# Weight slots of even attention and retention as 512-column pairs, a two-part gate product, and moved waits

## The reference, cut to what matters

```python
def even_layer(x, g_norm, w_in, b_f, w_out):
    z = rms_norm(x, g_norm) @ w_in
    ...
    log_f = jax.nn.log_sigmoid(fa.astype(f32) + b_f.astype(f32))
    ya = forgetting_attention(hA(qa), hA(ka), hA(va), log_f).reshape(Bsz, S, WIDTH_FOX)
    yb = dilated_attention(hB(qb), hB(kb), hB(vb)).reshape(Bsz, S, WIDTH_DIL)
    y = jnp.concatenate([ya * jax.nn.silu(ga), yb * jax.nn.silu(gb)], axis=-1)
    return x + y @ w_out

def odd_layer(x, g_norm, w_in, w_out):
    z = rms_norm(x, g_norm) @ w_in
    q, k, v, g = jnp.split(z, [qk_w, 2 * qk_w, 2 * qk_w + v_w], axis=-1)
    ...
    y = retention(q, k, v.reshape(Bsz, S, N_HEADS_RET, RET_V_DIM))
    y = head_group_norm(y).reshape(Bsz, S, v_w).astype(x.dtype)
    return x + (y * jax.nn.silu(g)) @ w_out
```

## Time and profile before

| | |
|---|---|
| runs, us | 1420.81, 1422.55, 1423.06 (median 1422.55) |
| the profiled execution's own time, us | 1422.35 |
| its span, first to last instruction, us | 1420.5 |
| mean granted TensorE clock | 0.994 |
| TensorE busy | 1374.0 us, 97% |
| VectorE, ScalarE, GpSimd busy | 976.5, 764.2, 96.6 us |
| weights loaded | 279 slots of 1 MB, median 4.9 us from issue to landing |

### The profile page before, as it was taken

The page is one execution under the profiler, slowest core; times in us unless marked ns, Lnnn a source line. Parts: engine busy times, 40 slices in busy tenths (PEclk is TensorE's granted clock), DMA queues, the critical chain, the costliest instruction groups (busy, mean ns, idle before and its releaser), DMA issues.

```text
span 1420.5 us, 22649 instructions
## 1 busy us (share of the span) xinstructions
PE 1374.0 (97%) x9089; PEld 1217.5 (86%) x9089; DVE 976.5 (69%) x1369; ACT 764.2 (54%) x927; POOL 96.6 (7%) x114
## 2 busy tenths in 40 slices
PE   7999999999999999999999999999999999999996
PEld 7998998789988889878999889887787888888884
DVE  6546566465766477866544475868887898898887
ACT  5545488334323317734433336743676677677673
POOL 0000032100001110001222010001000000000000
PEclk9999999999999999999999999999999999999998
DMA  7544333446543535534555535541898989889996
GB/s 272 216 161 144 123 145 137 161 149 216 199 149 119 212 136 181 178 120 173 193 190 185 181 147 215 180 159 54 334 347 303 347 327 345 334 327 351 335 335 248
DMA packets 44106, 306.36 MB, mean 216 GB/s; under 512 B 4912, under 2 KB 5168, under 8 KB 8176
## 3 DMA queue, kind: packets, MB, share of 16 engines
q1 hardware_dynamic: 41760, 296.22, 56.7%
q0 software_dynamic: 2256, 8.88, 1.8%
HBM read 304.03 MB, written 1.05 MB: 215 GB/s over the span
## 4 chain that ended last, share of the span: by engine, by line
PE 78%; DVE 10%; ACT 4%; DMA 4%; issue 3%; POOL 1%; DVEq 0%; SPq 0%; ACTq 0%
PE g_ps L585 18%; PE g_ps L587 18%; PE g_ps L586 18%; PE a_ps L585 5%; PE a_ps L587 5%; PE a_ps L586 5%; PE a_ps L590 4%; DMA raw<-w_dram 4%; DVE w_lo L1611 3%; ACT w_hi L1264 2%; PE a_ps L594 2%; PE o_ps L590 2%; DVE x L1742 1%; DVE tiny L1658 1%; POOL tiny L493 1%
## 5 line engine op out<-in xcount | busy, mean ns | idle before, releaser
L1611 DVE TENSOR_TENSOR w_lo<-raw,w_hi 128x2048 fp32r<-128x2048 f32 x239 | 546.3, 2289 | 226.1 <-ACT w_hi L1264 224.8
L1264 ACT ACTIVATE w_hi<-raw 128x2048 fp32r<-128x2048 f32 x239 | 457.3, 1914 | 259.7 <-DMA raw<-w_dram 101.8
L585 PE MATMUL g_ps<-x_hi,w_hi 128*128 128x256 f32 x880 | 252.2, 287 | 0.0
L586 PE MATMUL g_ps<-x_lo,w_hi 128*128 128x256 f32 x880 | 249.6, 284 | 0.0
L587 PE MATMUL g_ps<-x_hi,w_lo 128*128 128x256 f32 x880 | 249.5, 283 | 0.0
L585 PE MATMUL g_ps<-w_hi,x_hi 128*128 128x256 f32 (+1 forms) x672 | 230.5, 343 | 7.8 <-DVE w_lo L1611 3.9
L587 PE MATMUL g_ps<-w_hi,x_lo 128*128 128x256 f32 (+1 forms) x672 | 225.2, 335 | 0.0
L586 PE MATMUL g_ps<-w_lo,x_hi 128*128 128x256 f32 (+1 forms) x672 | 224.9, 335 | 0.0
L585 PEld LDWEIGHTS g_ps<-x_hi,w_hi 128*128 128x128 f32 x880 | 169.4, 193 | 4.0 <-issue 3.5
L586 PEld LDWEIGHTS g_ps<-x_lo,w_hi 128*128 128x128 f32 x880 | 169.5, 193 | 0.0
L587 PEld LDWEIGHTS g_ps<-x_hi,w_lo 128*128 128x128 f32 x880 | 169.4, 192 | 0.0
(11 more groups left out here) (326 smaller groups left out, 2043.4 us busy)
## 6 DMA issues: line engine op xcount, KB each, us to landing
raw<-w_dram SPq DMA_DIRECT2D x279, 1024.0 KB, 4.9
arena<-rows_dram POOLq DMA_DIRECT2D x3, 1024.0 KB, 5.1
arena<-xT_dram SPq DMA_DIRECT2D x2, 512.0 KB, 4.7
x<-x_dram SPq DMA_DIRECT2D x2, 512.0 KB, 10.4
extra<-extra_dram POOLq DMA_DIRECT2D x1, 1024.0 KB, 6.5
extra<-rows_dram POOLq DMA_DIRECT2D x2, 512.0 KB, 4.1
y_spare<-rows_dram POOLq DMA_DIRECT2D x4, 256.0 KB, 4.7
out_dram<-x SPq DMA_DIRECT2D x4, 256.0 KB, 2.1
```

The lines of the kernel that those rows point to most:

```text
L585: pe.matmul(ps, lh, rh, start=start, stop=False, skip_group_check=True)
L586: pe.matmul(ps, lh, rl, start=False, stop=False, skip_group_check=True)
L1264: act.activation(w_hi[w_place(s)][:, :], raw[PLACE[s]][:, :], ACT.Copy).then_inc(hi_done, 1)
L1611: dve.tensor_tensor(w_lo[w_place(s)][:, :], raw[PLACE[s]][:, :], w_hi[w_place(s)][:, :].bitcast(F32), ALU.subtract).then_inc(lo_done, 1)
```

## The change

It does these things:

- **Pairs.** Slots 20 to 23, 40 to 47 and 56 to 63 are laid out in DRAM as 4 x 128 rows by 512 columns (`wide_slots`), two slots a pair. `wide_slot(s, half)` uses one of them: for each of the two token tiles 4 x 3 matmuls of 512 columns, each tile into a bank of its own; a slot has 24 matmuls in place of 48. Both banks of a pair are copied after its second slot. For slots 40 and 41 both copies stand ahead of ScalarE's two splits; for later pairs the even slot's split stands ahead of the copies.
- **Retention.** VectorE takes a head's moments as soon as its output is there, then the next head's `decayed`, the norm, and only then the weight split and the gates; gates go in pairs, and each covers one token tile by 512 columns. `turn_outputs` waits for both gates of its pair.
- **Waits of attention.** The three waits ahead of each of the four attentions go; each pair of heads waits for the copy of its own K (and V) slot.
- **Narrow product.** It becomes `small_rows(0, 0)`: 32 matmuls of 128 columns with 48 or 24 weight columns, a copy of 48 rows by ScalarE (after `even_slot(3)`, ahead of `even_slot(4)`), and `fold_rows(0)` on TensorE between slots 4 and 5. VectorE splits slot 8 ahead of the log gates.
- **Start.** ScalarE runs a one-column copy before its first wait on a load.
- **Last mixer norm.** VectorE takes `low_part(5, 0)` after `finish(5, 1)`; TensorE has 8 filling matmuls and the transposes of tile 1 ahead of the first router part, where it had the part and 4 filling matmuls.
- **Loop counts.** `round_counts` moves from behind the split of slot 145 to right behind the first `select`; its one wide step stays behind.

```diff
+                         first=True, last=True, k_ready=copied(at_k + p // 2),
+                         v_ready=copied(at_v + p // 4 * 2 + 1 if b else p // 2)) for p in range(HF // 2)]
...
+            def wide_mm(s, half, t, ks):
+                w = weights(s + half, (4, 512))
+                for k in ks:
+                    mm = parts_mm(g_ps[bank_of(s + t)][:, :], pick(from_x, lambda u: u[:, k, t * P:(t + 1) * P]),
+                                  pick(w, lambda u: u[:, k - 4 * half, :]), k == 0, k == KD - 1)
+                return mm
+            def wide_free(s, t):
+                if g_nth[s + t] > 0:
+                    pe.wait_ge(g_free[bank_of(s + t)], g_nth[s + t])
+            def wide_slot(s, half):
+                pe.wait_ge(lo_done, s + half + 1)
+                for t in range(NT):
+                    if half == 0:
+                        wide_free(s, t)
+                    mm = wide_mm(s, half, t, range(4 * half, 4 * half + 4))
+                mm.then_inc(used, 1)
...
 begin(i, first), no second:
-                    first(0, every)
-                    keep_busy(4, 2, G_ALL)
+                    keep_busy(8, 2, G_ALL)
                     for b in range(2):
                         turn_rows_of(i, 1, b)
+                    first(0, every)
                 first(1, every)
...
-            narrow_product(0, HF)
-            for s in range(4, 8):
+            for t in range(NT):
+                small_rows(0, 0)(t, range(KD))
+            even_slot(4)
+            fold_rows(0)
+            for s in range(5, 8):
                 even_slot(s)
...
-            for s in range(9, 12):
-                pe.wait_ge(g_free[bank_of(s)], g_nth[s] + 1)
...
-                pe.wait_ge(r_y, b + 1)
+                pe.wait_ge(r_y, b - b % 2 + 2)
...
 ScalarE
+            act.wait_ge(pool_own, 3)
+            act.activation(tiny[:, 246:247], zero_col[:, :], ACT.Copy)
             act.wait_ge(ident_in, 16)
...
             for s in range(1, 4):
                 even_slot(s)
+            act.wait_ge(narrow_full, 1)
+            act.activation(rows24, a_ps[0][0:48, 0:S], ACT.Copy).then_inc(rows_copied, 1)
+            even_slot(4)
             act.wait_ge(f_in, 1)
...
             for m in range(8):
-                copy_slot(OD_V + m, rv[:, :, m * S:(m + 1) * S])
+                if m % 2:
+                    act.wait_ge(used, OD_V + m + 1)
+                    for t in range(NT):
+                        j = bank_of(OD_V + m - 1 + t)
+                        act.activation(rv[:, t, (m - 1) * S:(m + 1) * S], g_ps[j][:, :], ACT.Copy).then_inc(g_free[j], 1)
+                    for n in ((m - 1, m) if m == 1 else (m,)):
+                        ahead(OD_V + n)
+                elif m:
+                    ahead(OD_V + m)
...
 VectorE, rest_of_norm
-                low_part(i, 0)
+                if i < 5:
+                    low_part(i, 0)
                 centre(i, 1)
                 finish(i, 1)
+                if i == 5:
+                    low_part(i, 0)
...
 VectorE, retention
             for h in range(RH):
-                for u in G_AFTER[h]:
-                    ahead(OD_G + u)
-                    while gated <= u and gated < 2 * h:
-                        gate_slot(gated)
-                        gated += 1
+                dve.wait_ge(r_out, h + 1)
+                stats_of(lambda t: [a_ps[1 + t][:, :]], EPS)
                 if h < RH - 1:
                     decayed(h + 1)
-                dve.wait_ge(r_out, h + 1)
-                moments(lambda t: [a_ps[1 + t][:, :]], EPS)
                 y = inverse_root()
...
                 ins.then_inc(r_norm, 1)
+                for u in G_AFTER[h]:
+                    ahead(OD_G + u)
+                    while (gated | 1) <= u and gated < 2 * h + 2:
+                        gate_slot(gated)
+                        gated += 1
...
 VectorE, experts
                 select(slice(0, 2), 0)
+                round_counts()
                 ahead(L_WO[1] + 2)
```

More of the change, by code:

```diff
@@ L625, in rows_slot @@
                 mm.then_inc(used, 1)
[L627 to L641, removed]
             def out_mm(s, order, n, t, rows_ready=None):
@@ L686, in parts_come, with wide_part, part_of @@
                     pe.wait_ge(n_lo, 4 * i + 2 * t + k // 4 + 1)
+            def wide_mm(s, half, t, ks):
[14 more added lines that the diff above has]
+                mm.then_inc(used, 1)
+            def wide_part(i, s, half):
+                def part_of(t, ks):
+                    if t == 0 and ks[0] == 0:
+                        pe.wait_ge(lo_done, s + half + 1)
+                    if half == 0 and ks[0] == 0:
+                        wide_free(s, t)
+                    if ks[0] == 0:
+                        pe.wait_ge(n_lo, 4 * i + 2 * t + half + 1)
+                    mm = wide_mm(s, half, t, [4 * half + k // 2 for k in ks if k % 2 == 0])
+                    if t == 1:
+                        mm.then_inc(used, 1)
+                return part_of
             def token_part(i, s):
@@ L851, in even_slot @@
             def even_slot(s):
-                (token_slot if s in range(EV_V[0], EV_V[0] + 4) or s in range(EV_V[1], EV_V[1] + 4) else rows_slot)(s)
+                if s in range(EV_V[1], EV_V[1] + 4):
+                    wide_slot(s - s % 2, s % 2)
+                else:
+                    rows_slot(s)
             def plain_slot(s):
@@ L1331, in even_slot @@
                     ins = act.activation(gate_even(s - EV_G[0]), g_ps[bank_of(s)][:, :], ACT.Silu)
+                elif b and m >= 8:
+                    if s % 2:
+                        for t in range(NT):
+                            r = s - 1 + t
+                            ins = act.activation(qkv[1][2][t][:, (m - 8) // 2 * 512:(m - 8) // 2 * 512 + 512],
+                                                 g_ps[bank_of(r)][:, :], ACT.Copy)
+                            ins.then_inc(g_free[bank_of(r)], 1)
+                    ahead(s)
+                    return
                 elif s - EV_V[b] in range(4):
@@ L1395, in gate_slot @@
             def gate_slot(u):
-                s = OD_G + u
-                act.wait_ge(used, s + 1)
-                if u >= 3:
-                    act.wait_ge(r_y, u - 2)
-                act.activation(gate_view(s), g_ps[bank_of(s)][:, :], ACT.Silu).then_inc(g_free[bank_of(s)], 1)
-                ahead(s)
+                act.wait_ge(used, OD_G + u + 1)
+                for e in ((u - 1, u) if u % 2 else ()):
+                    s = OD_G + e
+                    if e >= 3:
+                        act.wait_ge(r_y, e - 2)
+                    act.activation(gate_view(s), g_ps[bank_of(s)][:, :], ACT.Silu).then_inc(g_free[bank_of(s)], 1)
+                ahead(OD_G + u)
             gate_slot(0)
```

81 lines of the change are left out of this document (35 added, 46 removed).

## The result

| | before | changed |
|---|---|---|
| runs, us | 1420.81 to 1424.99, median 1422.8 (4) | 1407.16 to 1410.64, median 1408.26 (4) |
| ratio | | 0.990, 95% interval 0.9884 to 0.9917 |
| the profiled execution's own time, us | 1422.35 | 1410.64 |

What follows compares the result with a forecast made beforehand. TensorE, with 78% of the chain, was taken to bound the kernel. Pairs 6.0 + retention 2.6 + attention waits 3.2 - start 1.9 + norm and experts 5.1 = 15.0 us faster: median 1407.4, own range 1404 to 1411.

Steps and rivals of the forecast that it cites:

- Pairs: Twenty slots as 512-column matmuls: 0.30 us saved a slot, 6.0 us in all, between 5.0 and 7.0.
- Rival 3: Pairs: width saves nothing, a matmul costs only its columns; 1.2 of 6.0 us remains, 1412 us; chance 0.05.
- No wait of TensorE at a pair's second tile: Sign for the pairs: TensorE never waits for the second tile's bank, since 12 matmuls (2.7 us) cover its copy.
- rival 4: Pairs: the bank of a pair's second tile is freed late, making the kernel slower, 1427 us at 2.0 a pair; chance 0.03.
- Retention, order: Retention stage: with moments ahead of VectorE's split, the waits before the second to fourth output products go, 1.7 us.
- Retention, odd output: End of retention: TensorE's 1.02 us wait for GpSimd's part of two outputs shrinks, 0.9 us gained.
- Waits of attention: Ahead of the four attentions: waits of 3.5 us go, a few tenths stay; 3.2 us gained, between 2.0 and 3.5.
- Start: Start up to slot 8: 1.9 us slower, with a 4.8 us wait before the fold and a clock fall costing 1.5.
- Rival 1: Start: ScalarE makes the 48-row copy in time, no new wait or clock fall; start gains 4.4, 1401 us; chance 0.08.
- The fall at 41.92: Start, kernel before: half clock for 3.41 us after 16-column matmuls, 1.7 us lost; should go with the narrow product.
- Norm, counts and experts: Last norm to slot 147: 0.4 us from the norm, 3.4 from an earlier load, 1.7 from the clock; 5.1 quoted.
- rival 2: Experts: loads at 0.95 share set the pace, about 1 of 5.1 us is kept, 1411.5 us; chance 0.14.

Runs made afterwards that it cites:

- c_after: The changed kernel itself, unaltered, measured once more in a second series against the kernel before: median 1408.28 us, ratio 0.989.
- after: The changed kernel as first measured against the kernel before: median 1408.26 us, ratio 0.990; its profiled execution took 1410.64 us.
- e6_narrow_v: Changed kernel with the retention's eight V slots (40 to 47) again as 48 matmuls of 256 columns, copied slot by slot: 1409.99 us, ratio 0.9903.
- e5_copies_first: Changed kernel with ScalarE's two copies of every retention V pair ahead of both the pair's splits: 1408.82 us, ratio 0.9883 to the kernel before.
- e4_old_order: Changed kernel with VectorE's old retention order, weight split and gates ahead of the decay and moments: 1412.78 us, ratio 0.9914 to the kernel before.
- e8_x_first: Changed kernel with ScalarE's 48-row copy ahead of `even_slot(2)`, and `x_hi` and the small weights' high part ahead of slot 4's split: 1403.38 us, ratio 0.9853.
- e2_counts_back: Changed kernel with `round_counts` back behind the split of slot 145: 1415.01 us, ratio 0.9925 to the kernel before.
- e9_casts_first: Changed kernel with VectorE's casts of the third and fourth gated output ahead of the weight split behind slot 62: 1408.38 us, ratio 0.9891.
- e1_rows_early: Changed kernel with ScalarE's 48-row copy ahead of `even_slot(3)`, so ahead of slot 7's split only: 1404.96 us, ratio 0.9857.

## Why the prediction was right, and where its steps were not

This table shows where TensorE's start times moved, from its timelines (us). The last column is what `c_after` gained on the kernel before since the row above; "behind the fourth attention" is the first `extra,arena` matmul after it:

| TensorE starts | before | `after` | `c_after` | gained |
|---|---|---|---|---|
| slot 8 | 67.62 | 71.46 | 69.68 | -2.06 |
| second attention | 184.93 | 185.77 | 183.99 | 3.00 |
| first V slot of the retention | 299.97 | 300.78 | 299.00 | 0.03 |
| first scores of the retention | 399.06 | 400.12 | 396.24 | 1.85 |
| odd output | 461.05 | 457.93 | 454.05 | 4.18 |
| fourth attention | 876.16 | 871.27 | 867.28 | 1.88 |
| behind the fourth attention | 924.82 | 920.38 | 916.78 | -0.84 |
| slot 143 | 991.96 | 987.19 | 983.60 | 0.32 |
| slot 147 | 1006.45 | 998.45 | 994.85 | 3.24 |
| (end of the span) | 1420.5 | 1408.7 | 1405.3 | 3.6 |

- **Pairs**, forecast 6.0: right. 0.28 a slot by `e6_narrow_v`, for 20 slots 5.6, less the waits of the V stage. By pitch, 0.120 us before and 0.227 now (325.19 to 327.69, eleven steps), it is 0.31; that 512-column matmuls come slower beside other work does not follow from the 240 instructions in 46.00 us, which are 0.19 us each. By the table it is nearer 0.34. Of the 3.00 up to the second attention 0.84 and 0.95 are waits that went, which leaves 1.2 for slots 20 to 23; the V slots gained 1.85 with a wait of 1.0 in it; and of the 4.18 up to the odd output 1.4 are waits, which leaves 2.8 for the gates. That is 5.8 net. Rival 3, with 1.2 of it left, falls.
- **"No wait of TensorE at a pair's second tile"**: wrong. 0.92 and a smaller one followed, by the mechanism of rival 4, though at two of ten pairs and with 1.3 us in all. The step that failed is "a staging place turns over in 9.2 us for two slots against 10.9", taken to mean that no split ahead of a copy waits for its load: a place does turn over in 9.1 us (on the chain one load begins at 312.60 and the next into its place at 321.66), but that load landed at 326.5, 1.3 us after the pair's end at 325.2, and the split ahead of the copies waited 4.43 us for it. `e5_copies_first` shows the copy's place to be the cause of the wait; why this load was late isn't shown. In `c_after` one of these waits is left, about 1.0 us.
- **Retention, order**, forecast 1.7: right; the three waits are gone, and `e4_old_order` brings larger ones.
- **Retention, odd output**, forecast 0.9 gained: wrong, 0.25 lost (1.27 for 1.02). I counted the gate (0.7) and the silu (0.6) that leave, and took the split for 2.29. It took 3.28. In the kernel before it began 3.31 us after GpSimd's low parts (455.00 and 451.69), when they were through; now it begins 1.53 us after them (451.51 and 449.98) and runs beside them. At 2.29 about 0.3 us of wait would be left.
- **Waits of attention**, forecast 3.2: right. The four waits ahead, 3.5, are gone, and 0.4 to 0.8 us of it comes back inside and behind the fourth attention (0.84 for 0.40 behind it, in `c_after` 0.70 there and 0.47 inside, for `stat`). That leaves 3.1 and 2.8.
- **Start**, forecast 1.9 lost, with a wait of 4.8 and one fall of the clock: right in mechanism, too small in size. The forecast's 67.1 and 66.7 for slot 8 both leave out what stands right ahead of it (67.62 before), which drops out of the difference. Slot 8 begins 2.1 us late in `c_after` (wait 4.1, one stretch at half clock) and 3.8 in `after` (wait 2.85, after a gate product that was itself 2.0 us late and fell to half clock, and then two stretches), and in the seven others between 2.1 and 3.8. What was too small is the clock's term: 1.5 us was forecast, and two stretches, 3.4 us, are the rule. The forecast had the gate product start as before; in nine of the eleven profiled executions with this order of ScalarE it starts 0.5 to 2.0 us behind slot 3, since `x_hi` stands behind the split of slot 4; with `e8_x_first` the gap is gone. Rival 1's price, 6.4 us between 1407.4 and 1401, is about what moving the copy gained (6.5).
- **The fall at 41.92** in the kernel before was put down to the 16-column matmuls, and it didn't come from a standstill: TensorE was busy in all of the stretch ahead of it.

```profile
38.51:41.92 3.41, 3.41 (x32) 3.41 (x33) 2.30 (x2) 0.00 (x0) 0.00 (x0) 1.00 0.64 233
```

- **Norm, counts and experts**, forecast 5.1: 5.3 in `c_after`, with 0.32 up to slot 143 (0.4 forecast), 3.24 up to slot 147 (3.4) and 1.7 for the fall at 1007.88, which went with the standstill; 4.85 by `e2_counts_back` for the counts alone. The load began at 984.66, 2.5 us ahead of slot 143. That the experts' loads would take the gain (rival 2, 0.14) did not happen.
- The edits of the last mixer norm and ScalarE's early table load were not tried alone.

**The sum owes something to luck.** The steps above make 13.2 us in `c_after`: 5.8, 1.4, 2.8, -2.1 and 5.3. Its profile is 15.2 us shorter than that of the kernel before. The other 1.9 lies behind slot 147 and is in no term of the forecast: there the profiled execution of the kernel before stood 1.00, 0.55 and 0.48 us at 1087.58, 1100.27 and 1106.85, where `c_after` has one wait of 0.96 (1091.96). Such groups of waits come and go: `e5_copies_first` and `e9_casts_first` have them, and take 414.7 and 412.6 us from slot 147 to the end, for 410.2 to 411.8 in the other changed kernels without a fall there; the kernel before takes 414.1, of which 1.7 is its fall. One profile of the kernel before can't tell whether this is its habit or its chance. With it the sum came within 1.2 us of both series, though the V stage (1.3), the odd output (1.2) and the start (0.2 to 1.9) were forecast too hopefully.

## What to carry to other kernels

When a result is handed over through another engine, look at what stands ahead of the handover in that engine's queue: if it waits for a load, the handover waits for the load too, and moving a 0.4 us copy two places up was worth as much as the twenty wider slots. Where one split that waits is found, check the one before it as well. And two-operand VectorE work costs more when GpSimd is moved beside it, so a reorder that frees one engine has to be priced with the overlap that it makes.

## What the runs showed of the hardware

VectorE and GpSimd held each other up. GpSimd's two `y_lo` ran 449.98 to 452.64 and VectorE's split, begun at 451.51, took 3.28 us for 2.29: 1.0 longer, about the 1.1 us that GpSimd still had to go. With the order reversed the split took 3.38 and GpSimd's second part 3.3 for 1.3, as if each got a full turn. The Trainium skill ("SBUF — State Buffer", Who interferes with whom) has it so: a VectorE instruction with two SBUF inputs contends with a GpSimd instruction that reads SBUF, and the ports that they share are an exclusive lock. These rows agree.

The same kernel doesn't always lose its clock in the same places. It fell near 301.70 in three of the fourteen profiled executions (`after`, `e1_rows_early` and `e6_narrow_v`), though all fourteen have the same idle time of 1.61 or 1.62 us ahead of it. The first profiled execution had 10.2 us more at half clock than that of `c_after`, and took 1410.64 us for 1407.39.
